# Mixture-of-experts layers: 128-token items with split float32r weights, against 32-token items with plain float32 weights on four column strips

## The reference, cut to what matters

```python
def hier_moe(xt, w_group, b_group, w_expert, b_expert, w1, w3, w2):
    glog = (xt @ w_group + b_group)                 # 4 groups, best one taken
    gprob = softmax(glog); g_sel = top1(glog); g_w = gprob[g_sel]
    elog_g = logits of the 8 experts of that group
    e_val, e_idx = lax.top_k(elog_g, 2)             # the two best experts
    weights = g_w * softmax(e_val)
    ...
    for every expert e and its tokens xb:
        hdn = jax.nn.silu(xb @ w1[e]) * (xb @ w3[e])    # 1024 -> 512
        ys = hdn @ w2[e]                                # 512 -> 1024
    y = sum over a token's two experts of weight * ys
```

## Time and profile before

| | us |
|---|---|
| median of three runs (4121.24 to 4124.8) | 4123.15 |
| the profiled execution, time | 4119.1 |
| its span, first to last instruction | 4117.3 |
| TensorE busy in it | 3435.0 |
| VectorE busy | 2301.4 |
| ScalarE busy | 1652.4 |
| mean granted TensorE clock, of full speed | 0.901 |

### The profile page before, as it was taken

The page is one execution under the profiler, slowest core; times in us unless marked ns, Lnnn a source line. Parts: engine busy times, 40 slices in busy tenths (PEclk is TensorE's granted clock), DMA queues, the critical chain, the costliest instruction groups (busy, mean ns, idle before and its releaser), DMA issues. The chain is left out here.

```text
span 4117.3 us, 45433 instructions
## 1 busy us (share of the span) xinstructions
PE 3435.0 (83%) x14888; PEld 2359.2 (57%) x14888; DVE 2301.4 (56%) x2639; ACT 1652.4 (40%) x1638; POOL 289.3 (7%) x393
## 2 busy tenths in 40 slices
PE   5499999999999974888888892899968489888882
PEld 0167757676776443666666771444425377766662
DVE  1413333333333345777777777455544577777777
ACT  0112222222222003666666663233311366666663
POOL 0000000000000102000000003000000200000002
PEclk7599989899985987999999995999989699999996
DMA  9522012102100426977887965200032597698895
GB/s 404 195 89 61 11 56 61 56 11 61 50 1 19 152 102 239 352 273 270 297 286 268 352 250 209 52 31 31 10 124 97 218 348 261 245 352 311 312 353 194
DMA packets 340697, 727.28 MB, mean 177 GB/s; under 512 B 74128, under 2 KB 110992, under 8 KB 334448
## 3 DMA queue, kind: packets, MB, share of 16 engines
q1 hardware_dynamic: 302960, 593.53, 41.9%
q10 hardware_dynamic: 19488, 70.46, 4.3%
q0 software_dynamic: 18144, 61.89, 4.1%
HBM read 626.04 MB, written 99.79 MB: 176 GB/s over the span
## 5 line engine op out<-in xcount | busy, mean ns | idle before, releaser
L1184 DVE TENSOR_TENSOR wlo<-raw,whi 128x2048 fp32r<-128x2048 f32 x488 | 1096.3, 2288 | 152.8 <-ACT whi L1136 152.8
L1136 ACT ACTIVATE whi<-raw 128x2048 fp32r<-128x2048 f32 x488 | 897.2, 1905 | 116.1 <-DMA raw<-in_moe_w 116.1
L84 PE MATMUL PS<-whi,xhi 128*128 128x512 f32 x1296 | 535.9, 413 | 58.0 <-DVE wlo L1184 45.4
L86 PE MATMUL PS<-whi,xlo 128*128 128x512 f32 x1296 | 513.3, 396 | 0.0
L85 PE MATMUL PS<-wlo,xhi 128*128 128x512 f32 x1296 | 513.2, 396 | 0.0
L84 PE MATMUL PS<-whi,hhi 128*128 128x512 f32 x640 | 260.9, 408 | 125.7 <-DVE hlo L1221 125.7
L84 PEld LDWEIGHTS PS<-whi,xhi 128*128 128x128 f32 x1296 | 244.4, 189 | 141.0 <-DVE wlo L1184 79.5
L648 PE MATMUL PS<-hT,slab 128*128 128x512 f32 (+1 forms) x768 | 303.0, 549 | 11.4 <-DMA slab<-in_na_w_qkv 7.3
L513 ACT ACTIVATE prob<-PS,small 128x768 f32<-128x768 f32 (+2 forms) x160 | 137.4, 859 | 407.9 <-DVE small L587 407.9
L86 PEld LDWEIGHTS PS<-whi,xlo 128*128 128x128 f32 x1296 | 244.4, 189 | 59.6
L682 PEld LDWEIGHTS PS<-V,probT 128*128 128x128 f32 x1792 | 247.0, 215 | 54.0 <-issue 41.0
(11 more groups left out here) (234 smaller groups left out, 4531.4 us busy)
## 6 DMA issues: line engine op xcount, KB each, us to landing
raw<-in_moe_w SPq DMA_DIRECT2D x412, 1024.0 KB, 7.7
aw<-in_ada_w SPq DMA_DIRECT2D x48, 1024.0 KB, 18.2
ys_d<-y ACTq DMA_DIRECT2D x80, 512.0 KB, 8.0
ys_d<-zero SPq DMA_DIRECT2D x8, 3584.0 KB, 14.2
slab<-in_na_w_qkv SPq DMA_DIRECT2D x24, 512.0 KB, 3.8
x_d<-x_p ACTq DMA_DIRECT2D x18, 512.0 KB, 4.8
h_d<-hb_p ACTq DMA_DIRECT2D x18, 512.0 KB, 2.6
xt_c<-x_d SPq DMA_DIRECT2D x18, 512.0 KB, 4.7
```

Source lines behind the costliest of these rows:

```text
L84: t.matmul(out_, lh, wh, start=start, stop=False)
L86: return t.matmul(out_, ll, wh, start=False, stop=stop)
L1136: a.activation(whi[(6 * j + q) % PARTS][:, :], raw[q % RAW][:, :], ACT.Copy).then_inc(hi_ok, 1)
L1184: v.tensor_tensor(wlo[r][:, :], raw[q % RAW][:, :], whi[r][:, :].bitcast(F32), ALU.subtract).then_inc(lo_ok, 1)
```

## The change

`routing` and `experts` become one block, `moe`, and the items, the arithmetic and the weights' path change:

- An item is 32 tokens of one expert, and every expert has at least two. With the router's counts these are 104 items in layer 0 and 100 in layer 1.
- A product is a plain float32 matmul with 32 stationary columns (tokens) and 256 moving columns (weights). Four of them, with different weight columns, write to the four 32-partition strips of one PSUM bank. Per item there are 8 steps of four for w1 and w3 (`up`) and 4 steps of four for w2 (`down`): 48 matmuls. `whi`, `wlo`, `xhi`, `xlo`, `hhi`, `hlo` and their instructions are gone.
- The host lays w1, w3 and w2 out for this (`strips`): six chunks of 1 MB an expert, each 128 partitions by 8 KB. Before, w1 and w3 came in runs of 2 KB and w2 in runs of 4 KB.
- `wt` is a ring of three whole experts. SP loads all six chunks of every expert once, also of one that has no tokens. It reloads a chunk when the item count `used[q]` says that the expert three places earlier is through with it.
- The order of the experts comes from a sort by item count, laid out so that large and small ones alternate. With the router's counts the items per expert are 10, 2, 2, 2, 7, 2, 2, 2, 7, ... in layer 0, and 8, 2, 2, 2, 7, ... in layer 1.
- The gather fetches quarters of rows (128 descriptors of 1 KB an item), and DVE transposes in 32x32 blocks (L1243, L1255); TensorE transposes nothing. The output is stored as 128 runs of 1 KB.
- The token lists come from one-hot matmuls (L1074: 160 in layer 0, 128 in layer 1) in place of the running sums on DVE, POOL's scatter and SP's load. The first two experts' weights are asked for when the tables of experts and bounds are ready (`tab_ok`), the third's when the token list is (`idx_ok`), since the routing's scratch lies in its buffer.
- `ys_d` has 4608 rows where it had 7168, so clearing it during attention writes less.

The core of the diff:

```diff
-MAX_ITEMS = EXPERTS + (2 * N - 1) // P
-ITEMS = 56
-SLOTS = ITEMS * P
+STRIP = 32
+ITEMS = 144
+SLOTS = ITEMS * STRIP
+NCH, CHUNK, WBUF = 6, 2048, 3
...
-def three(t, out_, lh, ll, wh, wl, start, stop):
-
-    t.matmul(out_, lh, wh, start=start, stop=False)
-    t.matmul(out_, lh, wl, start=False, stop=False)
-    return t.matmul(out_, ll, wh, start=False, stop=stop)
...
+                wt = [sbuf(st, f"wt{l}{b}", [P, NCH, CHUNK]) for b in range(WBUF)]
...
+                        def chunk(e, b, q):
+                            view = w13v[bass.ds(e, 1), q] if q < 4 else w2v[bass.ds(e, 1), q - 4]
+                            sp.dma_start(wt[b][:, q, :], view.rearrange("o p c -> (o p) c")).then_inc(w_in[b][q], 16)
+
+                        def reload(r, b):
+
+                            e = sp.value_load(ert[0:1, bass.ds(r, 1)], min_val=0, max_val=EXPERTS - 1)
+                            over = sp.value_load(bnd[0:1, bass.ds(r - 2, 1)], **span)
+                            for q in range(NCH):
+                                sp.wait_ge(used[q], over + (1 if q == NCH - 1 else 0))
+                                sp.sem_inc(sp_passed, 1)
+                                chunk(e, b, q)
...
+                        with g.Fori(0, count) as i:
+                            for j in range(2):
+                                g.wait_ge(xT_ok, 2 * i + j + 1)
+                                gather(2 * i + 2 + j, j)
...
+                        def tanh(n):
+
+                            a.wait_ge(used[3], n + 1)
+                            a.wait_ge(hid_ok, n + 1)
+                            a.activation(th[:, :], PS[:, UP, 0:P], ACT.Tanh, scale=0.5).then_inc(th_ok, 1)
+
+                        def store(n, i, j):
+
+                            a.wait_ge(used[5], n + 2)
+                            a.wait_ge(y_out[j], 16 * i + 16)
+                            a.activation(y[j][:, :], PS[:, DOWN, 0:QD], ACT.Copy).then_inc(y_ok, 1)
+                            a.wait_ge(y_ok, n + 2)
+                            a.dma_start(ys_d[bass.ds(n * STRIP, STRIP), :].rearrange("t (q c) -> q t c", q=4),
+                                        y[j][:, :]).then_inc(y_out[j], 16)
...
+                        def up(n, b, turn=None):
+
+                            t.wait_ge(xT_ok, n + 1)
+                            t.wait_ge(hid_ok, n + 1)
+                            for q in range(4):
+                                if turn is not None:
+                                    t.wait_ge(w_in[b][q], 16 * turn + 16)
+                                for c in range(2):
+                                    k = 2 * q + c
+                                    for g in range(4):
+                                        mm = t.matmul(PS[32 * g:32 * g + 32, UP, 0:QD], xT[:, k * 32:k * 32 + 32],
+                                                      wt[b][:, q, c * 1024 + g * QD:c * 1024 + g * QD + QD],
+                                                      start=(k == 0), stop=(k == KD - 1))
+                                mm.then_inc(used[q], 1)
...
+                        def expert(r, b, turn, lo, hi):
+
+                            first = turn if b < WBUF - 1 else turn + 1
+                            with t.Fori(lo + 1, hi) as n:
+                                up(n, b)
+                                down(n - 1, b, turn)
+                            up(hi, (b + 1) % WBUF, first)
+                            down(hi - 1, b)
+
+                        t.wait_ge(tab_ok, 1)
+                        up(0, 0, 0)
+                        with t.Fori(0, EXPERTS // WBUF) as i:
+                            for b in range(WBUF):
+                                lo = t.value_load(bnd[0:1, bass.ds(WBUF * i + b, 1)], min_val=0, max_val=ITEMS - 2)
+                                expert(WBUF * i + b, b, i, lo, bound(WBUF * i + b + 1))
...
+                        rows_T(0, 0, 0)
                         with v.Fori(0, count) as i:
                             for j in range(2):
                                 n = 2 * i + j
...
+                                v.wait_ge(used[3], n + 1)
                                 rows_T(n + 1, 1 - j, i + j)
...
+                                hidden(n)
```

More of the change, by code:

```diff
@@ L120, in program @@
         h2_d = dram("h2_d", (N, D))
-        slot_d = [dram(f"slot_d{l}", (P * ITEMS, 1), I32) for l in range(2)]
         ys_d = dram("ys_d", (SLOTS, D))
@@ new lines, in moe @@
+                rows_in, tab_ok, idx_ok = nm("rows"), nm("tab"), nm("idx")
+                w_in = [[nm(f"w{b}{q}") for q in range(NCH)] for b in range(WBUF)]
+                used = [nm(f"used{q}") for q in range(NCH)]
+                y_out = [nm(f"y_out{j}") for j in range(2)]
+                g_in = [gather_sem(f"rows{j}_m{l}") for j in range(2)]
+                ib_ok, xT_ok, th_ok, u_ok, hid_ok, hT_ok, y_ok = (nm(x) for x in ("ib", "xT", "tanh", "u", "hid", "hidT", "y"))
+                passed, a_passed, sp_passed = nm("passed"), nm("act_passed"), nm("sp_passed")
@@ new lines, in _ @@
+                        for b in range(WBUF):
+                            e = sp.value_load(ert[0:1, b:b + 1], min_val=0, max_val=EXPERTS - 1)
+                            if b == WBUF - 1:
+                                sp.wait_ge(idx_ok, 1)
+                            for q in range(NCH):
+                                chunk(e, b, q)
+                        with sp.Fori(1, EXPERTS // WBUF) as i:
+                            for b in range(WBUF):
+                                reload(WBUF * i + b, b)
@@ new lines, in _ @@
+                        t.wait_ge(g_ok, 1)
+                        t.matmul(PS[:, 1, 96:128], spread(bcol), H[e32, :], start=True, stop=True).then_inc(b_ok, 1)
+                        for k in range(2):
+                            t.wait_ge(o_ok, k + 1)
+                            for a_ in range(k * nt, k * nt + nt):
+                                for g in range(4):
+                                    mm = t.matmul(PS[32 * g:32 * g + 32, 2, 0:ITEMS], OHt[:, a_, :], OHi[:, a_, :],
+                                                  start=(a_ == 0), stop=(a_ == NA - 1))
@@ new lines, in down @@
+                        def down(n, b, turn=None):
+                            t.wait_ge(hT_ok, n + 1)
+                            t.wait_ge(y_ok, n + 1)
+                            for q in range(4, 6):
+                                if turn is not None:
+                                    t.wait_ge(w_in[b][q], 16 * turn + 16)
+                                for c in range(2):
+                                    k = 2 * (q - 4) + c
+                                    for g in range(4):
+                                        mm = t.matmul(PS[32 * g:32 * g + 32, DOWN, 0:QD], hT[:, k * 32:k * 32 + 32],
+                                                      wt[b][:, q, c * 1024 + g * QD:c * 1024 + g * QD + QD],
+                                                      start=(k == 0), stop=(k == KF - 1))
+                                mm.then_inc(used[q], 1)
@@ new lines, in _ @@
+                        t.wait_ge(tab_ok, 1)
+                        up(0, 0, 0)
+                        with t.Fori(0, EXPERTS // WBUF) as i:
+                            for b in range(WBUF):
+                                lo = t.value_load(bnd[0:1, bass.ds(WBUF * i + b, 1)], min_val=0, max_val=ITEMS - 2)
+                                expert(WBUF * i + b, b, i, lo, bound(WBUF * i + b + 1))
+                        R = EXPERTS // WBUF * WBUF
+                        for r in range(R, EXPERTS):
+                            lo, hi = bound(r), bound(r + 1)
+                            if r + 1 < EXPERTS:
+                                expert(r, r - R, EXPERTS // WBUF, lo, hi)
+                            else:
+                                with t.Fori(lo + 1, hi) as n:
+                                    up(n, r - R)
+                                    down(n - 1, r - R, EXPERTS // WBUF)
+                                down(hi - 1, r - R)
+                                t.wait_ge(used[3], hi)
+                                t.wait_ge(used[5], hi + 1)
@@ L1782 @@
     arrays, aps = {}, {}
-    for name in _INS:
-        a = np.ascontiguousarray(inputs[name])
+    stacked = strips(inputs["moe_w1"], inputs["moe_w3"], inputs["moe_w2"])
+    for name in _INS + list(stacked):
+        a = np.ascontiguousarray(stacked[name] if name in stacked else inputs[name])
         if name == "na_rpb":
```

538 lines of the change are left out of this document (215 added, 323 removed).

## The result

The changed kernel takes 3829.7 us (median of 4 runs, 3795.5 to 3861.2) against 4122.8 (4121.2 to 4124.8) before. The ratio is 0.921 (95% interval 0.919 to 0.923). It is faster by 7.9%, and slower than the whole forecast range of 3480 to 3720 us. The median lies between two groups of runs, 3795 to 3801 and 3859 to 3861 us; the ratio is that of the first group, and experiment 10 shows what parts them: a stretch of attention at full or at half clock, so that at like clock the gain is 6.1 to 6.4%.

The account below looks back on a forecast made before the run. The MoE stages were taken as bound by TensorE, DVE close behind. Stages of 642 and 623 us against 960.9 and 867.6 save 563.5 of 4119.1, giving 3555.6; with the median 4 us above, 3560. Range 3480 to 3720 us, 78%.

Parts of the forecast that it names:

- Gather and store have two items, 10.3 us: MoE items: a gather or store lands in at most 10 us, which fits under two items of TensorE work.
- The term for transfers: MoE stages: each item's gather and store add 0.75 us of DMA work, 78 us for 104 items.
- The last sentence of the prediction: Sign of being wrong: DMA share under 0.85 with TensorE waiting, as a chain between items taken as hidden then binds.
- late gathers: Rival: gathers take 18.2 us as a 1 MB share did, an item 9.75 us, about 4390 us; chance 4%.
- Transfers: MoE weights, gathers and stores: 555 us of DMA work in layer 0, 552 in layer 1; 28 idle, 7 behind in layer 0.
- TensorE: MoE matmuls: four strips side by side, 5.15 us an item, 536 us for layer 0 and 515 for layer 1.
- two queues that don't hide each other: Layer 0: transfers (590) and TensorE (595) nearly equal, so 17 us were added, giving 612.
- The head: Routing at the start of layer 0's stage: tables at 24 us, counting matmuls 7.4 us, first `up` at about 52 us.
- The rest of the program: Everything outside the two MoE stages: taken as unchanged, 2290.6 us.
- Weight loads show: Rival: loads stand between TensorE's matmuls, an item takes 7.8 us, the kernel 4060 us; chance 6%.
- the instruction stream: Rival: TensorE's sequencer needs 56 ns an instruction, an item takes 10.8 us, the kernel 4600 us; chance 7%.
- The loop's jump: Rival: each of nine outer-loop jumps a layer idles TensorE 6.5 us, 59 us a layer, the kernel 3660 us; chance 10%.

Follow-up runs that it names:

- experiment 10: Kernel of experiment 2 plus a second clearing of the same size in attention, into a buffer nothing reads: 3449.7 us once, five runs of 3499 to 3511.
- experiment 2: Changed kernel with each item's store split into four DMAs, one for each strip, same bytes and two buffers: 3501.9 us (median of 4).
- experiment 6: Kernel of experiment 2 with every second matmul of an item left out, so that only transfers can bind: 3413.4 us (one run).
- experiment 5: Changed kernel, but after each layer's first three experts a weight chunk brings one run of 8 KB instead of 128: 3509.9 us (one run).

## Why the prediction was right or wrong

**The step that failed** is in the part on TensorE: "Gather and store have two items, 10.3 us", landing "at most 10, which just fits, and less with a quarter of the bytes". It took landing times of DMAs spread over sixteen engines for a store with another pattern, and looked at bytes where the outermost dimension decides. In place of at most 10 us the store that leaves at 1575.91 us has not landed before 1597 us, 21 us later, and on end the stores pass only every 11 us where an item takes 5.2. The store before had its rows outermost, the new one its four strips; both stand in the code, and the step compared only sizes. The term for transfers has the same fault: 0.75 us an item is right for sixteen engines, but each of the four has 32 x 0.049 = 1.6 us of store packets an item beside the gather. The last sentence of the prediction named the sign (a DMA share under 0.85 together with a waiting TensorE, now 0.78) and the cause (a chain between items that had been taken as hidden). It had no chance of its own. The only rival near it, late gathers, concerned the other DMA of an item: it is not what binds, since DVE never waits for a gather inside layer 0 of experiment 2 but for the first.

**With that one fault mended the rest can be read**, on experiment 2: layers of 615.2 and 592.2 us where 642 and 623 had been worked out.

- *Transfers.* Layer 0 was put at 24 + 555 + 7 us without idle time; transfers alone take 592.0 us (experiment 6), 581.2 in layer 1, at 408 GB/s and a share of 1.00. The size was right. The gather's part of it has another make than the text has it: the trace shows it as 32 packets of 4 KB an item, 0.16 us each, and not as 128 of 1 KB. By their share of the engines' time (6.4% of 500 us for 92 gathers in experiment 2) that is 0.35 us an item on each engine, where the sums of the experiments took 0.37.
- *TensorE.* `up` follows `up` in 5.18 us, 5.15 forecast: four strips side by side, and their loads hidden. In layer 0 of experiment 2 the time behind the first `up` is 571.5 us; 536 + 31 + 17 + 6 = 590 was forecast. Most of the excess is the 17 us for two queues that don't hide each other: experiment 5, with no weights to wait for, is within 3 us of number 2. So TensorE binds, by 20 us in layer 0 and 13 in layer 1.
- *The head.* Tables at 20 us (24), first `up` at 44 (52). The counting matmuls took 5.5 us, not 7.4, and the 160 matmuls of the lists 7.7 us.
- *The rest of the program* was taken as unchanged. It is, but for a clock that moves by itself, by 50 to 60 us in the last pair of heads. That is more than the range allowed for anything outside the stages.

**The rivals.** *Weight loads show* and *the instruction stream* are out: eight loads begin within 0.23 us, and a step of 16 records keeps its 0.43 us for whole items (nor does it take the 0.50 us that the prediction estimated from the figure of the Trainium skill for hardware decoding off; no row shows whether it is off). The first step of the first item of experiment 2, loads and then matmuls:

```profile
1573.20 0.23 PEld L1091 LDWEIGHTS PS<-wt,xT 128*32 128x32 f32 x8 [9.91 <-issue]
1573.23 1.08 PE L1091 MATMUL PS<-wt,xT 128*32 128x256 f32 x8 [9.65 <-DVE xT L1244]
```

The rule of the Trainium skill quoted there for the first ("TensorE: Matmul & The Clock Gate", "The mechanism") would have made an item 7.8 us, by the rows' price of a load; the measured 5.18 decides against it for column strips that use all rows. The same section of the Trainium skill also lets a load pass that goes to the background weight buffer, which the prediction left out; no run here shows which of the two buffers a load goes to.

*The loop's jump* is out as a cost of 6.5 us; it is 0.5. The loop over three experts starts again at every third change of expert. In experiment 5, where neither weights nor stores hide it, TensorE idles 0.74 to 0.82 us at every third change and 0.24 to 0.30 at nearly all the others. The first such jump, between the third and the fourth expert:

```profile
1655.66 3.66 PE L1090 MATMUL PS<-wt,xT 128*32 128x256 f32 x64 [0.82 <-issue]
```

Ten turns of the loop have nine jumps, so they cost some 5 us a layer, where the rival had 59.

*Low clock*: 0.90 from the first to the last weights in the changed kernel, 0.98 in experiment 2. The lower value is a result of the waits, not their cause.

## What to carry to other kernels

Before costing a DMA, write down its outermost dimension on both sides: a landing time from the trace holds for another DMA only if both are spread over as many engines, and a store whose pattern starts with a dimension of 4 can make four engines the bound of everything that shares them. When a chain between two engines is taken as hidden with almost no margin (10 of 10.3 us), it is a case with a chance and a price, not a sentence in the sum. And before the rest of a program is taken as unchanged, see whether its clock is the same in several executions.

## What the runs showed of the hardware

- A store of 128 runs of 1 KB spread over four engines passes only every 11 us while 8 KB packets of another queue are waiting, though its packets take 49 ns. Over sixteen engines it lands in 7.4 us beside the same weights. The layer took 897, 788 and 615 us on two, four and sixteen engines, all with two buffers.
- Four strips of 32 columns run side by side without loss: 16 records of TensorE (8 loads and 8 matmuls) in 0.43 us, one in 27 ns, for items on end.
- The same 435 matmuls of attention ran at full clock in some executions of the same kernel and at half in others, 73 or 131 us, with the same idle time of 1.47 us ahead of them. In attention the full clock ended after 113 to 116 us time after time, and what differed was whether one of these falls came. No run here shows what decides it.
